# One core, two transformer layers: rotary keys transposed once, output weights packed, top-2 by ranks, last rows scaled by ScalarE

## The chip, the core and the metric

The kernel runs on one core of a Trainium2 chip. The metric is the device time of one execution in microseconds (us); less is better. PE is TensorE, ACT ScalarE, DVE VectorE, POOL GpSimd, and SP the engine that here only issues DMAs (SPq is its queue). Everything is float32 but for a few exact bf16 tables of the routing.

## The reference

640 token rows (128 context rows, then 512 latent rows) of 1024 columns pass two layers. What matters here, cut from the reference:

```python
def mix(qs, kvs, w_uk, w_uv, lam_p, diff_g, lam_init, w_out):
    k_nope = jnp.einsum('bkr,rhd->bkhd', ckv, w_uk)                    # 6 heads x 32
    k_a = jnp.concatenate([k_nope, jnp.broadcast_to(k_rope[:, :, None, :], ...)], axis=-1)  # + the same 32 for all heads
    ...                                                                # three kinds of attention
    return jnp.einsum('bse,ed->bsd', o, w_out)

def hier_moe(h, w_grp, b_grp, w_rtr, b_rtr, w_gate, w_up, w_down):
    g_top, g_idx = lax.top_k(jax.nn.softmax(t @ w_grp + b_grp), 1)     # one of 4 groups
    e_sel = ...                                                        # the 4 logits of that group
    e_top, e_idx = lax.top_k(jax.nn.softmax(e_sel), 2)                 # two of its 4 experts
    ...                                                                # 16 experts of 1024 -> 256 -> 1024
def block(...):
    mod = silu(cond) @ w_mod[i] + b_mod[i]                             # shift1, scale1, gate1, shift2, scale2, gate2
    h = rms_norm(x, norm1_g[i]) * (1 + scale1) + shift1
    x = x + gate1 * mix(...)
    h = rms_norm(x, norm2_g[i]) * (1 + scale2) + shift2
    x = x + gate2 * hier_moe(h, ...)
```

## The kernel before

Rows are worked on in NT = 5 tiles of 128. Each layer has five stages, written out by hand in program order for every engine, with semaphores between them.

1. **Projection** (`z_block`, `hT_round`, `keys1`, `keys2`). Per tile PE transposes the normalised rows (8 transposes, bank 7 of PSUM, L1799) and multiplies by `w_in` in four column blocks (L1907). Per unit of 128 keys (2 cached units and 5 of the tiles) `keys1` makes 4 transposes into bank 4, ACT copies them out (`key_copies_a`, L957 and L958), and `keys2` makes, for each of 3 head pairs, one product of `wuk` with the compressed keys (L1862) and one product of the raw key columns with the identity (L1863) that adds the rotary part in the same accumulation; ACT copies this out with one instruction of 128 partitions (L964).
2. **Attention**: scores, exponentials, transposes, values, by 10 map pairs per tile. Beside it PE makes the 8 later chunks of the modulation (`mod_chunk`, L1824) from 2 MB blocks of `w_mod`.
3. **Output projection** (`out_block`, L2098), in three column blocks of `w_out` per tile, with the residual add (`x_add`), the second norm (`mixer_in`) and the router logits. DVE's `mixer_in_last` makes the last tile's normalised rows (L1521), which POOL stores to `h_rows` in DRAM (L841).
4. **Routing**, on DVE: from the 20 logits per row the group, two experts, counts, ranks, slots (L1585 to L1680), with small products on PE in between. POOL then gathers the first 128 rows of `h_rows` (L893). In layer 0 PE also makes the four first modulation chunks of layer 1 and transposes their result (`mod_T`, L1840): chunks 0 and 1 ahead of the routing's counts, chunks 2 and 3 behind them, and then `mod_T`, ahead of the product that gives the slots (L2196).
5. **Experts**: steps of 128 gathered rows, 29 over both layers, of one expert or of two (gate and up L2248 to L2254, down L2289 to L2296). POOL adds each result to `x_rows` with a scatter that accumulates (L879), one at a time.

SBUF for weights is the `ring`, four slots of 2 MB, and the `arena`. SP issues all weight DMAs in one order (the list `USES`), each after a wait on what used the slot before (`slot_free`). Slot 3 also holds probabilities during attention. The three `w_out` blocks take slots 2, 0 and 1, one each; so chunk 0 of layer 1's modulation goes to slot 3 when attention is done, and chunks 1, 2 and 3 to slots 2, 0 and 1 as the last tile has used each `w_out` block. Experts 0 and 1 follow the chunks that they replace; experts 2 and 3 wait for the first gather besides. Softmax denominators of attention travel through DRAM (`fac_rows`) and come back, broadcast, into `q_tok[1]` or arena columns 4096 to 5120 (`factors_of`).

## Time and profile before

| what | value |
|---|---|
| time, median of 3 runs | 1405.07 us (1403.48 to 1409.73) |
| the profiled execution's own time | 1402.38 us |
| its span in the profile | 1400.6 us |
| mean granted clock of TensorE | 0.955 of full |
| PE busy | 1239.2 us, 88% of the span |
| DVE busy | 719.1 us, 51% |
| ACT busy | 412.7 us, 29% |
| POOL busy | 233.3 us, 17% |
| DMA | 250.48 MB, mean 179 GB/s |

The stages by the profile's clock: layer 0's projection runs from about 42 to 195 us, attention to 392, output projection to 473, routing to 506, experts to 717; layer 1's from 727 to 882, to 1076, to 1159, to 1185, and to the end. A busy share says how much an engine worked, not whether anyone waited for it. A busy engine in a stage of 99% is that stage's bound; in the routing all engines are mostly idle, and there the chain of waits tells what counts.

### The profile page before, as it was taken

What the parts mean: (1) busy time and instruction counts of PE and PEld (TensorE: products, weight loads), DVE (VectorE), ACT (ScalarE), POOL (GpSimd) and SP (SyncE); (2) the same over time, 40 slices, a digit from 0 to 9 for tenths busy, and PEclk for the clock granted to TensorE, in tenths of its full rate; (3) what the DMA queues carried; (4) which work ended last, traced back from release to release, by engine and by line L of the source; (5) the groups of instructions that cost most, each with busy time, mean ns of one, the idle gap of its engine ahead of it and who ended that gap; (6) DMA issues with size and microseconds to landing.
All of it is one profiled execution on the core that took longest, in us unless ns stands there. A gap on an engine that the chain in (4) does not pass through costs nothing.

```text
span 1400.6 us, 22064 instructions
## 1 busy us (share of the span) xinstructions
PE 1239.2 (88%) x7898; PEld 725.4 (52%) x7898; DVE 719.1 (51%) x1728; ACT 412.7 (29%) x931; POOL 233.3 (17%) x335
## 2 busy tenths in 40 slices
PE   4999999999989869988959999899998993999980
PEld 3455556767756534433435554676666662444330
DVE  0344436777834625553514453567786445455442
ACT  2111145766611201111111111567665110111101
POOL 1220021110121112211111001211111111111212
PEclk9899999999999979999969999999999996999995
DMA  9800188010052887999950005760113344899955
GB/s 346 303 15 1 62 302 240 17 47 17 16 177 80 318 358 262 351 375 358 312 174 14 1 1 180 271 153 16 48 31 97 130 153 167 325 372 367 336 179 181
DMA packets 75625, 250.48 MB, mean 179 GB/s; under 512 B 6551, under 2 KB 15392, under 8 KB 62896
## 3 DMA queue, kind: packets, MB, share of 16 engines
q1 hardware_dynamic: 56080, 183.26, 35.1%
q0 software_dynamic: 18976, 63.94, 15.9%
q8 instruction: 99, 1.62, 0.5%
q10 hardware_dynamic: 432, 1.36, 0.2%
q14 instruction: 38, 0.31, 0.1%
HBM read 219.12 MB, written 31.08 MB: 179 GB/s over the span
## 4 chain that ended last, share of the span: by engine, by line
PE 63%; DMA 20%; DVE 7%; issue 6%; DVEq 1%; ACT 1%; POOL 1%; SPq 0%; POOLq 0%; ACTq 0%
PE ps L1907 17%; DMA x_rows<-arena,idx 13%; PE ps L2098 10%; PE ps L1799 8%; PE ps L1981 8%; PE ps L2254 5%; PE ps L2034 5%; PE ps L1824 2%; PE ps L2296 2%; PE ps L2248 2%; DVE ring L1362 2%; DMA ring<-in_w_mod 2%; DMA ring<-in_w_in 1%; DMA x<-in_x_sample 1%; DMA hT_region<-h_rows,idx 1%
## 5 line engine op out<-in xcount | busy, mean ns | idle before, releaser
L1907 PE MATMUL ps<-ring,hT_region 128*128 128x512 f32 (+1 forms) x640 | 270.3, 578 | 3.4 <-ACT hT_region L990 3.4
L1907 PEld LDWEIGHTS ps<-ring,hT_region 128*128 128x128 f32 x640 | 120.9, 192 | 134.4 <-issue 133.9
L1362 DVE TENSOR_SCALAR_CACHE_REDUCE ring<-ps 128x768 f32<-128x768 f32 (+1 forms) x168 | 132.7, 820 | 95.5 <-PE ps L1981 77.6
L1044 ACT ACTIVATE ring<-ring,negm 128x768 f32<-128x768 f32 (+1 forms) x168 | 137.6, 820 | 26.8 <-DVE ring L1362 26.8
L2098 PE MATMUL ps<-ring,hT_region 128*128 128x384 f32 (+1 forms) x480 | 143.5, 454 | 0.0
L2254 PE MATMUL ps<-ring,hT_region 128*128 x272 | 127.2, 623 | 10.3 <-SPq L600 4.3
L1981 PE MATMUL ps<-arena,qT 64*128 64x384 f32 (+1 forms) x640 | 124.8, 507 | 8.5 <-DVE ring L1362 4.1
L2098 PEld LDWEIGHTS ps<-ring,hT_region 128*128 128x128 f32 x480 | 89.2, 190 | 42.9 <-issue 1.5
L2034 PE MATMUL ps<-work,arena 128*64 128x128 f32 x1600 | 105.0, 278 | 5.6 <-ACT work L1060 4.3
L1060 ACT ACTIVATE work<-ps 128x512 f32<-128x512 f32 x128 | 75.8, 592 | 89.1 <-PE ps L1799 89.1
L2034 PEld LDWEIGHTS ps<-work,arena 128*64 128x64 f32 x1600 | 85.9, 136 | 24.6 <-issue 14.3
L2248 PE MATMUL ps<-ring,hT_region 128*64 x192 | 88.2, 614 | 9.8 <-SPq L600 9.8
L879 POOL DMA_INDIRECT x_rows<-arena,idx x29 | 47.9, 1652 | 293.9 <-DVE arena L1771 205.1
L2254 PEld LDWEIGHTS ps<-ring,hT_region 128*128 128x128 f32 x272 | 53.4, 199 | 80.6 <-issue 80.6
L1149 ACT ACTIVATE work<-ps 128x256 f32<-128x256 f32 x29 | 11.2, 384 | 281.8 <-PE ps L2254 158.9
L1758 DVE COPY work<-ps 128x256 f32<-128x256 f32 x29 | 12.3, 424 | 158.9 <-PE ps L1799 158.9
L2249 PE MATMUL ps<-ring,hT_region 128*64 128x512 f32 x192 | 88.3, 614 | 0.0
L1799 PE MATMUL ps<-ident,ring 128*128 128x128 f32 x600 | 81.9, 278 | 0.3
L1799 PEld LDWEIGHTS ps<-ident,ring 128*128 128x128 f32 x600 | 65.2, 140 | 28.0 <-issue 25.1
L1981 PEld LDWEIGHTS ps<-arena,qT 64*128 64x128 f32 (+1 forms) x640 | 56.1, 185 | 41.7 <-issue 15.0
L1237 DVE TENSOR_TENSOR work<-ps,rope 128x256 f32<-128x256 f32 (+2 forms) x40 | 14.0, 350 | 114.4 <-PE ps L1907 113.5
L1824 PE MATMUL ps<-ring,silu_c 128*2 128x128 f32 x1536 | 51.0, 290 | 19.9 <-DMA ring<-in_w_mod 19.2
(305 smaller groups left out, 1724.3 us busy)
## 6 DMA issues: line engine op xcount, KB each, us to landing
ring<-in_w_mod SPq DMA_DIRECT2D x24, 2048.0 KB, 10.5
ring<-in_moe_w_gate SPq DMA_DIRECT2D x32, 1024.0 KB, 11.6
ring<-in_moe_w_up SPq DMA_DIRECT2D x32, 1024.0 KB, 15.2
arena<-in_moe_w_down SPq DMA_DIRECT2D x32, 1024.0 KB, 14.3
ring<-in_w_in SPq DMA_DIRECT2D x6, 2048.0 KB, 20.2
arena<-mod_rows POOLq DMA_DIRECT2D x12, 512.0 KB, 5.7
arena<-fac_rows POOLq DMA_DIRECT2D x20, 256.0 KB, 4.4
x_rows<-x POOLq DMA_DIRECT2D x10, 512.0 KB, 3.1
```

The lines of the kernel that those rows point to most:

```text
L1044: act.activation(v, v, ACT.Exp, bias=negm[:, 2 * (k % 3) + m:2 * (k % 3) + m + 1], scale=-1.0, accum_out=sums[:, c:c + 1]).then_inc(exp_do ...
L1060: act.activation(to[:, 512 * b:512 * (b + 1)], ps[:, 4 + b, :], ACT.Copy).then_inc(pt_evac[b], 1)
L1362: ts(o_, i_, -pair_of(p)[4], None, ALU.mult, ALU.min, accum_out=col).then_inc(m_ready, 1)
L1799: return pe.transpose(out, in_, ident[:])
L1824: last = mm(ps[32 * h:32 * h + 2, mod_bank(j), mod_cols(j)], silu_v[:, :, c], w[:, c, 128 * h:128 * (h + 1)], start=(c == 0), stop=(c == K ...
L1907: last = mm(ps[:, b, 0:n], hT[:, c, t * P:(t + 1) * P], w[:, c, :], start=(c == 0), stop=(c == KC - 1))
L1981: last = mm(ps[:, 2 * m + c, 0:384], q[r:r + n, :], kT[r:r + n, plane, 384 * c:384 * (c + 1)], start=True, stop=True)
L2034: last = mm(ps[64 * m:64 * (m + 1), 7, (u % 4) * P:(u % 4 + 1) * P], V[:, s_, vc:vc + 64], w[:, 768 * m + c * P:768 * m + (c + 1) * P], st ...
L2098: last = mm(ps[:, n % 4, 0:w_], oT[:, c, t * P:(t + 1) * P], w[:, c, :], start=(c == 0), stop=(c == KC - 1))
L2248: mm(g[0:HALF], h[:, c, 0:HALF], wa[:, c, :], start=(c == 0), stop=(c == KC - 1))
L2249: last = mm(g[HALF:P], h[:, c, HALF:P], wb[:, c, :], start=(c == 0), stop=(c == KC - 1))
L2254: last = mm(g, h[:, c, :], wa[:, c, :], start=(c == 0), stop=(c == KC - 1))
```

## The change

- **Rotary transposes joined.** `keys1` makes a fifth transpose, of the raw key columns with the rotary part, into bank 7; `key_copies_a` writes it to all three head pairs with two ACT copies of 32 partitions (rows 32 and 96), and a new semaphore `kr_evac` guards bank 7 ahead of `hT_round`. The three identity products of `keys2` are gone. `key_copies_b` copies the product's rows 0 and 64, 32 partitions each, where it was one copy.
- **Output weights packed.** The three `w_out` blocks lie one behind the other in slots 0 and 1. Slot 2 is free once attention's chunks are done, slot 3 with attention's end. `LATE`, the order in which experts take slots, is now 2, 3, 0, 1. Layer 1's chunks 0 to 3 lie in slots 2 and 3 and in two places of the arena (`mod_home`) that held keys, values and queries. Factors come back to the last 1024 columns of the weights for the keys (`factors_of`), and small tiles of the router move to make room.
- **Loads.** `first_experts` replaces the list's order: gate and up of expert 2 after the next-to-last block of the output projection; experts 0 and 1 after chunks 0 and 1 (in layer 1: expert 0's gate and up before attention ends, the rest of 0 and 1 at its end); expert 2's down and all of 3 after the first gather, as before.
- **Top-2 by ranks.** Each set of 4 logits is compared with itself, all pairs at once (25 sets x 16 = 400 elements), against a table `above` made once, and the sum gives each logit's place. The gate weights are computed behind the expert table and no longer ahead of it. A running sum (one `tensor_tensor_scan`) replaces product and reduction over 16 x 16.
- **Last rows.** `mixer_in_last` is gone. POOL writes the shift row (`b2b`) to the last tile of `h_rows` early; ACT scales the last rows; POOL adds them to that tile in DRAM with an accumulating DMA, ahead of the last `x_store`.

The diff, cut:

```diff
+        uses += [("out", l, b, b) for b in range(len(WO_COLS))]
+            uses += [("mod", l + 1, j, (2, 3, 1, 0)[j]) for j in range(MOD_FIRST)]
...
+        def wo_block(b):
+            return ring[:, WO_AT[b]:WO_AT[b] + KC * (WO_COLS[b][1] - WO_COLS[b][0])].rearrange("p (c n) -> p c n", c=KC)
+        def mod_home(l, j):
+            if l >= 1 and j in (2, 3):
+                return arena[:, DN0 + 4096 * (3 - j):DN0 + 4096 * (4 - j)]
+            return slot[USES[USE_AT["mod", l, j]][3]]
...
+                elif kind == "mod" and l >= 1:
+                    if i == 0:
+                        sp.wait_ge(mod_done, l * N_MOD - 2)
+                    else:
+                        sp.wait_ge(pv_done, l * NUT)
...
 for t in range(NT):
+                    if t == 1:
+                        pool.wait_ge(s_bcast, (l + 1) * 32)
+                        dma(h_rows[NT * P:(NT + 1) * P, :], b2b[:, 1, :]).then_inc(s_hout, 16)
...
+                pool.wait_ge(h2_ready, l * NT + NT)
+                dma(h_rows[NT * P:(NT + 1) * P, :], h2, accum_op=ALU.add).then_inc(s_hout, 16)
                 x_store(NT - 1)
-                h2_store(NT - 1)
                 pool.wait_ge(idx_ready, l + 1)
-                pool.wait_ge(s_hout, l * 80 + 80)
+                pool.wait_ge(s_hout, l * 96 + 96)
...
 def key_copies_a(l, u):
+                for r in (32, 96):
+                    last = act.activation(kT[r:r + 32, 0:3, KCOL[u]:KCOL[u] + P],
+                                          ps[r:r + 32, 7, 0:P].unsqueeze(1).to_broadcast([32, 3, P]), ACT.Copy)
+                last.then_inc(kr_evac, 1)
 def key_copies_b(l, u):
-                act.activation(kT[:, 0:3, KCOL[u]:KCOL[u] + P],
-                               ps[:, 5, 0:384].rearrange("p (j n) -> p j n", j=3), ACT.Copy)
+                for r in (0, 64):
+                    act.activation(kT[r:r + 32, 0:3, KCOL[u]:KCOL[u] + P],
+                                   ps[r:r + 32, 5, 0:384].rearrange("p (j n) -> p j n", j=3), ACT.Copy)
...
+                act.wait_ge(lg_ready, l * NT + NT)
+                act.wait_ge(s_hout, l * 96 + 16 * NT)
+                act.activation(h2, last_scaled, ACT.Copy, scale=rs2[:, NT - 1:NT]).then_inc(h2_ready, 1)
                 act.wait_ge(r_sub, 2 * l + 1)
                 act.activation(r_gex, r_gs, ACT.Exp).then_inc(r_exp, 1)
-                act.wait_ge(r_sub, 2 * l + 2)
-                act.activation(r_ex2, r_d, ACT.Exp).then_inc(r_exp, 1)
                 if l + 1 < DEPTH:
                     for j in range(MOD_FIRST):
                         mod_copy(l + 1, j)
+                act.wait_ge(r_sub, 2 * l + 2)
+                act.activation(r_ex2, r_d, ACT.Exp).then_inc(r_exp, 1)
...
+                tt(beats, four.unsqueeze(2).to_broadcast([P, blocks_, 4, 4]),
+                   four.unsqueeze(3).to_broadcast([P, blocks_, 4, 4]), ALU.subtract)
+                tt(beats, beats, above[:]..., ALU.is_ge)
+                red(v3(r_place, 4), beats, AX.X, ALU.add)
+                ts(r_first, r_place, 0.0, None, ALU.is_equal)
+                ts(r_second, r_place, 1.0, None, ALU.is_equal)
...
+                dve.tensor_tensor_scan(r_incl, ones[:, 0:NE], r_nt, 0.0, ALU.mult, ALU.add)
...
 def keys1(l, u):
+                pe.wait_ge(kr_evac, l * NU + u)
+                if u == 0 and l >= 1:
+                    pe.wait_ge(a1_ready, l + 1)
+                tr(ps[:, 7, 0:P], kt[:, 128:256])
 def keys2(l, u):
                 for j in range(3):
-                    mm(ps[:, 5, j * P:(j + 1) * P], wuk[:, j * P:(j + 1) * P], ckvT[:], start=True, stop=False)
-                    mm(ps[:, 5, j * P:(j + 1) * P], kt[:, 128:256], ident[:], start=False, stop=True)
+                    mm(ps[:, 5, j * P:(j + 1) * P], wuk[:, j * P:(j + 1) * P], ckvT[:], start=True, stop=True)
 def hT_round(t, r):
+                    if r == 0:
+                        pe.wait_ge(kr_evac, l * NU + (t + 1 if t or l else 2))
```

How the order moves. First PE in the projection of layer 0, over one key unit: `keys1` (four L1799 on `pack`, between two blocks), then `keys2`. Before:

```order
L1799 MATMUL ps<-ident,pack 128x128 x4
L1907 MATMUL ps<-ring,hT_region 128x416 x8
L1799 MATMUL ps<-ident,work 128x128 x4
L1907 MATMUL ps<-ring,hT_region 128x512 x8
L1862 MATMUL ps<-ckvT,pack 128x128
L1863 MATMUL ps<-ident,pack 128x128
L1862 MATMUL ps<-ckvT,pack 128x128
L1863 MATMUL ps<-ident,pack 128x128
L1862 MATMUL ps<-ckvT,pack 128x128
L1863 MATMUL ps<-ident,pack 128x128
L1864 MATMUL ps<-pack,ckvT 128x384
```

And after the change, the same stretch (L1838 is the transpose, L1949 the block, L1903 and L1904 are `keys2`):

```order
L1838 MATMUL ps<-ident,pack 128x128 x5
L1949 MATMUL ps<-ring,hT_region 128x416 x8
L1838 MATMUL ps<-ident,work 128x128 x4
L1949 MATMUL ps<-ring,hT_region 128x512 x8
L1903 MATMUL ps<-ckvT,pack 128x128 x3
L1904 MATMUL ps<-pack,ckvT 128x384
```

Of each unit three of the seven products of `keys2` are gone, and `keys1` has five transposes where it had four. Second, SP's queue in layer 0 from `w_out` to the experts, with its waits. Before:

```order
L657 DMA ring<-in_w_out 128x2x256
L603 DMA ring<-in_w_mod 128x8x512 [waits pv_done,z_done]
L603 DMA ring<-in_w_mod 128x8x512 [waits wo_done] x3
L575 DMA ring<-in_moe_w_gate 128x2048 [waits mod_done]
L575 DMA ring<-in_moe_w_up 128x2048
L579 DMA arena<-in_moe_w_down 128x2048 [waits pv_done]
L575 DMA ring<-in_moe_w_gate 128x2048 [waits mod_done]
L575 DMA ring<-in_moe_w_up 128x2048
L579 DMA arena<-in_moe_w_down 128x2048
L575 DMA ring<-in_moe_w_gate 128x2048 [waits experts_ready,wgu_landed0,wd_landed0,wgu_landed1,wd_landed1,mod_done,s_hg0_0]
L575 DMA ring<-in_moe_w_up 128x2048
L579 DMA arena<-in_moe_w_down 128x2048
```

After the change:

```order
L617 DMA ring<-in_w_mod 128x8x512 [waits w_landed2,mod_done]
L617 DMA ring<-in_w_mod 128x8x512 [waits pv_done]
L617 DMA arena<-in_w_mod 128x8x512 [waits w_landed1,pv_done]
L617 DMA arena<-in_w_mod 128x8x512 [waits w_landed0,pv_done]
L589 DMA ring<-in_moe_w_gate 128x2048 [waits wo_done]
L589 DMA ring<-in_moe_w_up 128x2048
L589 DMA ring<-in_moe_w_gate 128x2048 [waits mod_done]
L589 DMA ring<-in_moe_w_up 128x2048
L589 DMA ring<-in_moe_w_gate 128x2048 [waits mod_done]
L589 DMA ring<-in_moe_w_up 128x2048
L593 DMA arena<-in_moe_w_down 128x2048 [waits mod_done]
L593 DMA arena<-in_moe_w_down 128x2048
```

The loads of chunks 1 to 3 no longer wait for the output projection (`wo_done`), expert 2's gate and up stand ahead of expert 0's, and the two downs behind both. Third, DVE in the routing of layer 0, from the last step of the selection to the counts. Before:

```order
L1604 TENSOR_TENSOR arena<-arena 128x5x4x4 x2
L1607 TENSOR_TENSOR arena<-arena 128x80
L1609 TENSOR_TENSOR arena<-lane 128x256
L1521 SCALAR_TENSOR_TENSOR work<-arena,small 128x1024
L1614 TENSOR_SCALAR arena<-ps 128x16
L1616 TENSOR_SCALAR arena<-arena 128x16
L1619 TENSOR_TENSOR arena<-arena 128x256
L1621 TENSOR_SCALAR arena<-arena 128x8
L1622 TENSOR_SCALAR arena<-arena 128x8
L1624 TENSOR_REDUCE arena<-arena 128x16
L1626 CAST arena<-arena 128x8
```

After the change, the whole selection from its first instruction (L1627) to the running sum (L1653) that stands for L1619 and L1624:

```order
L1627 TENSOR_TENSOR arena<-work 128x400
L1630 TENSOR_TENSOR arena<-arena,above 128x400
L1633 TENSOR_REDUCE arena<-arena 128x100
L1635 TENSOR_SCALAR arena<-arena 128x100
L1636 TENSOR_SCALAR arena<-arena 128x100
L1640 TENSOR_TENSOR arena<-arena 128x5x4x4 x2
L1643 TENSOR_TENSOR arena<-arena 128x80
L1645 TENSOR_REDUCE arena<-work 128x5
L1647 TENSOR_TENSOR arena<-work,arena 128x20
L1649 TENSOR_SCALAR arena<-ps 128x16
L1651 TENSOR_SCALAR arena<-arena 128x16
L1653 SCALAR_TENSOR_TENSOR arena<-ones,arena 128x16
```

The 1024-column instruction L1521 is gone from this queue. Ahead of the mask's sum (L1607 before, L1643 now) the selection has seven instructions, three of which read 400 elements; before it had 22, of 5 to 80 elements.

## Rows read from the trace of the kernel before

**Rows 1.** The chain that ended last: shares of the span by engine.

```profile
PE 63%; DMA 20%; DVE 7%; issue 6%; DVEq 1%; ACT 1%; POOL 1%; SPq 0%; POOLq 0%; ACTq 0%
```

**Rows 2.** Windows: from:to, length, busy per engine (count), PE clock, DMA share, GB/s.

```profile
60.00:195.00 135.00, 133.47 (x468) 68.35 (x470) 64.44 (x215) 19.66 (x56) 19.02 (x26) 1.00 0.18 62
398.00:473.00 75.00, 74.04 (x352) 50.46 (x352) 33.33 (x55) 9.40 (x20) 13.13 (x26) 1.00 0.38 133
483.00:493.00 10.00, 6.04 (x96) 4.63 (x90) 6.08 (x29) 2.16 (x8) 0.15 (x1) 0.81 1.02 423
...
600.00:700.00 100.00, 87.30 (x333) 35.94 (x330) 47.69 (x69) 13.53 (x20) 16.47 (x13) 0.97 0.98 349
...
1168.00:1177.00 9.00, 0.78 (x15) 0.46 (x11) 7.86 (x35) 0.00 (x0) 0.53 (x1) 0.50 0.16 61
```

**Rows 3.** Timeline (start us, length us, engine, line), PE, `keys2` of one unit.

```profile
179.84 0.38 PE L1862 MATMUL ps<-ckvT,pack 128*128 128x128 f32 x2
...
180.06 0.39 PE L1863 MATMUL ps<-ident,pack 128*128 128x128 f32 x2
```

**Rows 4.** Timeline, PE: twelve transposes of attention in one row.

```profile
374.87 1.53 PE L1799 MATMUL ps<-ident,ring 128*128 128x128 f32 x12
```

**Rows 5.** Timeline, PE and ACT, projection of layer 0: `keys1` to `hT_round`.

```profile
78.47 0.60 PE L1799 MATMUL ps<-ident,pack 128*128 128x128 f32 x4
...
79.28 0.48 ACT L958 ACTIVATE arena<-ps 128x384 f32<-128x384 f32 x1
...
79.66 1.06 ACT L950 ACTIVATE work<-x 128x1024 f32<-128x1024 f32 x1
...
84.50 0.60 PE L1799 MATMUL ps<-ident,work 128*128 128x128 f32 x4
```

**Rows 6.** Timeline, DVE, the routing of layer 1.

```profile
1161.35 0.24 DVE L1539 SCALAR_TENSOR_TENSOR work<-ps,small,pack 128x20 f32<-128x20 f32 x1 [0.98 <-POOL small L722]
...
1167.08 0.24 DVE L1607 TENSOR_TENSOR arena<-arena 128x80 bf16<-128x80 f32 x1
...
1168.78 0.17 DVE L1614 TENSOR_SCALAR arena<-ps 128x16 f32<-128x16 f32 x1
...
1169.27 0.43 DVE L1619 TENSOR_TENSOR arena<-arena 128x256 f32<-128x256 f32 x1
...
1170.41 0.17 DVE L1626 CAST arena<-arena 128x8 int32<-128x8 f32 x1
...
1176.86 0.18 DVE L1680 SCALAR_TENSOR_TENSOR idx<-arena,w_slot 128x18 int32<-128x18 f32 x1
```

**Rows 7.** Chain (start us, length us, what), the first gather of layer 1.

```profile
1177.32 4.36 DMA hT_region<-h_rows,idx
```

**Rows 8.** Line 879, scatters that add: issue to landing.

```profile
DMA to landing us min/median/max: 6.0/10.8/12.1
```

**Rows 9.** Line 841, plain stores of rows: issue to landing.

```profile
DMA to landing us min/median/max: 2.9/2.9/8.6
```

**Rows 10.** Timeline, SP queue, layer 0: chunks 1 to 3, then expert 0.

```profile
460.41 11.49 SPq L603 DMA_DIRECT2D ring<-in_w_mod  x3
475.85 0.35 SPq L575 DMA_DIRECT2D ring<-in_moe_w_gate  x1
```

**Rows 11.** Chain, the routing of layer 0, to the first expert step.

```profile
485.70 3.51 PE ps L1824 x64
...
490.40 1.05 PE ps L1840 x8
...
493.80 8.63 DMA hT_region<-h_rows,idx
...
506.58 3.54 PE ps L2254 x4
```

**Rows 12.** Timeline, DVE and PE, routing of layer 0: last logits, then chunk 2.

```profile
474.56 0.24 DVE L1539 SCALAR_TENSOR_TENSOR work<-ps,small,pack 128x20 f32<-128x20 f32 x1 [0.98 <-POOL small L722]
...
481.19 1.93 PE L1824 MATMUL ps<-ring,silu_c 128*2 128x128 f32 x64
```

More of the change, by code:

```diff
@@ L85 @@
 WO_COLS = [(0, 384), (384, 768), (768, 1024)]
+WO_AT = [KC * c0 for c0, _ in WO_COLS]
 RING = 4
@@ L154 @@
 USE_AT = {u[:3]: g for g, u in enumerate(USES)}
-SLOT_AT = {u[:3]: u[3] for u in USES}
-USE_BEFORE = [max((h for h in range(g) if USES[h][3] == u[3]), default=None) for g, u in enumerate(USES)]
 USE_CUM = [16 * sum({"moe": 0, "out": 4}.get(v[0], 1) for v in USES[:g + 1] if v[3] == u[3])
@@ L1464, in _ @@
                     if t == NT - 1:
+                        if p == 0 and l == 0:
+                            rank_table()
                         if p == 1:
@@ new lines, in _ @@
+                four = logits.rearrange("p t n -> p (t n)").rearrange("p (b n) -> p b n", n=4)
+                beats = r_big[:, 0:blocks_ * 16].rearrange("p (b i j) -> p b i j", i=4, j=4)
+                tt(beats, four.unsqueeze(2).to_broadcast([P, blocks_, 4, 4]),
+                   four.unsqueeze(3).to_broadcast([P, blocks_, 4, 4]), ALU.subtract)
+                dve.drain()
+                tt(beats, beats, above[:].rearrange("p (i j) -> p i j", i=4).unsqueeze(1).to_broadcast([P, blocks_, 4, 4]),
+                   ALU.is_ge)
@@ new lines, in _ @@
+                dve.drain()
+                red(v3(r_place, 4), beats, AX.X, ALU.add)
+                dve.drain()
+                ts(r_first, r_place, 0.0, None, ALU.is_equal)
+                ts(r_second, r_place, 1.0, None, ALU.is_equal)
+                dve.drain()
+                first, second = (v.rearrange("p (t b n) -> p t b n", t=NT, n=4) for v in (r_first, r_second))
+                for o_, O_ in ((first, r_O1), (second, r_O2)):
+                    tt(O_.rearrange("p (t e g) -> p t g e", t=NT, e=EPG), o_[:, :, 1:, :],
+                       first[:, :, 0, :].unsqueeze(3).to_broadcast([P, NT, NGRP, EPG]), ALU.mult)
@@ L1606, in _ @@
-                dve.drain()
-                tt(r_Mb, r_O1, r_O2, ALU.add).then_inc(r_mask, 1)
-                tt(r_le.rearrange("p (e s) -> p e s", e=NE), lane[:, 0:NE].unsqueeze(2).to_broadcast([P, NE, NE]),
-                   lane[:, 0:NE].unsqueeze(1).to_broadcast([P, NE, NE]), ALU.is_ge)
-                mixer_in_last()
+                tt(v3(r_gs, 4), G, r_gm.unsqueeze(2).to_broadcast([P, NT, 4]), ALU.subtract).then_inc(r_sub, 1)
                 dve.wait_ge(r_count, l + 1)
@@ L1703, in _ @@
                    ).then_inc(experts_ready, 1)
+                for k, O_ in enumerate((r_O1, r_O2)):
+                    tt(r_sel[:, 80 * k:80 * (k + 1)].rearrange("p (t e g) -> p t g e", t=NT, e=EPG),
+                       E.rearrange("p t (g e) -> p t g e", g=NGRP),
+                       O_.rearrange("p (t e g) -> p t g e", t=NT, e=EPG), ALU.mult)
+                dve.drain()
+                red(r_m, v3(r_sel, NE), AX.X, ALU.add)
+                dve.drain()
+                tt(r_d, r_m[:, NT:2 * NT], r_m[:, 0:NT], ALU.subtract).then_inc(r_sub, 1)
+                dve.wait_ge(r_exp, 2 * l + 1)
+                red(r_gtop, v3(r_gex, 4), AX.X, ALU.add)
+                dve.wait_ge(r_exp, 2 * l + 2)
+                ts(r_den, r_ex2, 1.0, None, ALU.add)
                 dve.drain()
```

205 lines of the change are left out of this document (95 added, 110 removed).

## The prediction

> **What bounds the kernel now.** I read the chain that ended last first: PE holds 63% of it and DMAs 20% [rows 1]. Then the windows, stage by stage [rows 2]. In layer 0's projection PE is busy 133.47 of 135 us, in the output projection 74.04 of 75: there every product that goes is time that goes. In the output projection the DMA engines are at 0.38, so loads fit in. The routing is the opposite: in 9 us of layer 1's routing PE works 0.78 us and DVE 7.86, at a granted clock of 0.50, the lower of the two levels (1.2 GHz), after PE had gone idle. There the length of DVE's chain is the time. In layer 0's routing the DMA engines are full too (1.02, 423 GB/s), with PE busy 6.04 of 10 us at 0.81. In the experts stage PE is busy 87.30 of 100 us and the DMA engines 0.98: both are near their limit.
>
> **Rotary transposes.** In `keys2` a pair of records starts every 0.22 us [rows 3]; three identity products are 0.66 us a unit. What comes is one transpose: twelve take 1.53 us with a tail of about 0.28, so (1.53 - 0.28) / 11 = 0.11 us each [rows 4]. Net 0.55 us a unit. Units 0 and 1 of layer 0 lie ahead of the first block, which waits for weights, and unit 0 of layer 1 under the load of x; that leaves 5 + 6 = 11 units in a PE-bound stretch: -6.1 us. The new copies are ACT's, which is busy 19.66 of 135 us [rows 2]. A copy of as many columns (384) takes 0.48 us [rows 5]; I take 32 partitions for no cheaper than 128. After `key_copies_a` two more end at about 79.76 + 2 x 0.48 = 80.7 us, and the next user of bank 7, `hT_round`, starts at 84.50 [rows 5]: 3.8 us of cover, which a block of `w_in` gives. Behind them on ACT the square sum (79.66, 1.06 us) starts 0.9 us later; it is for the tile after next. If ACT were late, PE would stand at every unit.
>
> The Trainium skill (TensorE: Matmul & The Clock Gate, Part 4: PE-mode transpose) gives about 275 ns for a transpose in one kernel's context. This trace has records of that length but starts them every 0.11 us [rows 4]; by the page's figure the net would be 0.39 us a unit and the sum 1.8 us smaller.
>
> **Routing, layer 1.** From the start of the last logits instruction to the end of the mask's sum (L1607) are 1167.32 - 1161.35 = 5.97 us [rows 6], of which 0.33 is the first instruction. The new selection: a 256-element instruction takes 0.43 us, and a small one 0.17 [rows 6], so 400 elements are about 0.43 + 144 x 1.1 ns = 0.58. Three of these, each with 0.07 for the drain, 1.95; two of 100 elements 0.36; two of 80 0.47; the sum 0.24: 3.0 us against 5.64, so -2.6. Then L1609 and L1521 stood ahead of the counts, which begin 1168.78 - 1167.32 = 1.46 us behind the mask [rows 6]; now two small ones stand there and PE's five small products, about 0.5: -1.0. From the counts to the cast 1170.41 - 1168.78 = 1.63 us go to product, reduction and four small ones [rows 6]. The trace has no running sum; bounds are a small instruction (0.17) and a 256-element one (0.43). I take 0.2, since it has 16 elements: 0.94 in all, -0.7, ends -0.7 and -0.4. Joining two products and two reductions gives -0.1. Together **-4.4 us**. Behind the expert table DVE has about 1.6 us more for the weights; the gather's 4.36 us [rows 7] and PE's transposes cover it, with some 0.7 us to spare.
>
> The last rows now go ACT, POOL, DMA. ACT can start at 1161.6, takes about 1.06 (1024 columns, [rows 5]), and POOL issues near 1163.0. No row shows a plain add into DRAM. Nearest are the scatters that add: 6.0 us at the least, 12.1 at the most [rows 8]; a plain store needs 2.9, and 8.6 under load [rows 9]. The DMA engines are nearly idle here, so I take 6.0: landed at 1169, ahead of the gather's new issue at 1177.3 - 4.4 = 1172.9. With 12.1 it would cost 2.2 us. It can't gain.
>
> **Routing, layer 0.** SP issued chunks 1 to 3 from 460.41 to 471.90 [rows 10], 6.3 MB, and experts 0 and 1, 6.3 MB, from 475.85. Chunk 3's products could therefore start only at 485.70, `mod_T` at 490.40, and the gather was issued at 493.80 [rows 11]. Now the chunks are loaded as attention ends, some 60 us early, while PE has the output projection. Next in line: the mask at 474.56 + 0.33 + 3.0 = 477.9 [rows 12], `r_gs` and its exponential 0.6, the copy of chunk 0 (about 1.1), chunk 2 (1.93, [rows 12]), chunk 3, its copy: `mod_T` starts near 484.9, -5.5 us, and still ends behind DVE's tables (-4.4). So the gather is issued near 488.3. It took 8.63 us here against 4.36 in layer 1 [rows 7, 11]. From 475.85 on there are 6.3 MB of experts 0 and 1 and four row tiles of 0.5 MB, 8.4 MB, at 420 GB/s [rows 2] 20 us: about 495.9. Between 492.7 (4.36) and 496.9 (8.63) I take 495.9, near the loaded row. Before, it had landed at 502.43: **-6.5 us**, ends -5.5 and -9.8. The adding DMA is issued near 476.2; with 12.1 us it lands at 488.3, just in time.
>
> The Trainium skill (DMA: Bandwidth & Descriptors, Queues, rings and completion order) says that an engine takes turns between queues packet by packet. By that what counts is whether the weights' queue has work, not how much: the gather would keep its 8.63 us, and the sum be 1.0 us smaller.
>
> **The rest.** Expert 2's gate and up are loaded before the routing, but PE reached step 2 without waiting, so I cost this at nothing; steps follow at PE's pace. The packed `w_out` does not change a product. The table of ranks is two small instructions in late attention, with what DVE delays there +0.3 us. More bytes early in the output projection (6.3 MB in layer 0, 4.2 in layer 1, 10 to 15 us) lie beside the factors' return; cover is PE's 74 us.
>
> Sum: -6.1 - 4.4 - 6.5 + 0.3 = **-16.7 us**. The profiled execution's own time of 1402.4 gives 1385.7; it is 2.7 us under the median of 1405.07, so for the median I say **1388.4 us**.
>
> **Rivals.**
> 1. *Bytes bind the experts.* For it: DMA share 0.98 at 349 GB/s [rows 2]. Then layer 0 gains the 6.3 MB that leave the crowded time, 18 us, and layer 1 another 2.1 MB, 6 us, in place of 6.5 and 4.4: 1388.4 - 13.1 = 1375. Against it: PE is busy 87.30 of the same 100 us.
> 2. *Routing half won.* The adding DMA needs 12 us in layer 1 and more in layer 0, where stores triple under load [rows 9], and the gather waits for it: 2.2 and about 4 us lost, 1394.6.
> 3. *The joined transposes don't shorten the projection*, since PE waits for ACT at bank 7. The 3.8 us of cover speak against it. Without the 6.1 us: 1394.5.
> 4. *Slower: the adding DMA is late in both layers.* With a landing L after issues at 476.2 and 1163.0, the gathers move by 2L - (493.8 - 476.2) - (1177.3 - 1163.0) = 2L - 31.9 us. With the other terms (-5.8) it is slower from L = 18.9; L = 24 gives +10.3, 1415. For it: a read, an add and a write of DRAM, beside full engines in one layer. Against it: 12.1 is the longest of 29 [rows 8].
>
> **How the numbers follow.** Forecast 0.70, rival 1 0.08, rival 2 0.13, rival 3 0.05, rival 4 0.04. A measurement tells 0.5%, 7 us, from no change. The forecast's own ends: routing of layer 0 -9.8 gives 1385, the transposes' page figure, 12.1 in layer 1 and the running sum's 0.3 and 1.0 for layer 0's gather give 1393.7. Rivals 2 and 3 reach from 1394 to 1397 with part of each other, rival 1 halfway 1380; the range is 1380 to 1397. Over 7 us faster: forecast, rival 1 and most of 2 and 3, 0.88. Within: 0.08, the rest of them. Slower: 0.04.
>
> **What would show it.** Right: projection stages each about 3 us shorter with PE still at 99%; no DMA wait ahead of chunk 3; counts about 3.6 us sooner behind the last logits; the gather in layer 1 issued 4.4 us sooner; experts stages as long as before. Wrong: PE waiting on ACT ahead of `hT_round`; POOL's gather released by the adding DMA rather than by DVE; an experts stage that changes its length by several us.

## The result and the profile after

The changed kernel took **1390.37 us** (median of 4 runs, 1387.05 to 1392.83), the kernel before beside it 1404.28 us. The ratio is 0.9893, 95% interval 0.9868 to 0.9917: 13.9 us faster, by more than the 0.5% that a measurement can tell. The prediction was 1388.4 us, 1380 to 1397.

The profiled execution took 1392.47 us, of which the span is 1390.7. I cut the span at the first product of each stage, and at the end of the last tile's last output block. "Again" is the same changed kernel, profiled a second time (e9_again below). All numbers are durations in us between two such starts in the timeline:

| stretch | before | after | again |
|---|---|---|---|
| start to first `w_in` block | 42.62 | 43.04 | 42.94 |
| layer 0: projection, to the first wide scores | 171.99 | 172.74 | 168.80 |
| rest of attention | 177.83 | 179.58 | 178.19 |
| output projection, to the end of its last block | 78.90 | 78.58 | 78.68 |
| routing, to the first expert product | 35.24 | 29.72 | 30.03 |
| experts | 220.94 | 219.60 | 222.26 |
| layer 1: projection and attention | 352.80 | 349.04 | 349.14 |
| output projection | 77.81 | 77.66 | 77.64 |
| routing | 27.21 | 22.80 | 22.72 |
| experts and end | 215.26 | 217.94 | 218.10 |

Read it downwards: both routings became shorter, and so did the projections, but for layer 0's in the first execution; layer 1's experts became longer in both executions. In layer 0's projection and attention the two executions of one and the same kernel differ by 5.3 us.

The chain of waits of the changed kernel, its share by engine; it answers to [rows 1]:

```profile
PE 71%; DMA 13%; DVE 6%; issue 5%; ACT 1%; DVEq 1%; POOL 1%; SPq 1%; POOLq 0%; ACTq 0%
```

A key unit in the projection, timeline (start us, duration, engine, line, operation, tiles):

```profile
79.54 0.71 PE L1838 MATMUL ps<-ident,pack 128*128 128x128 f32 x5
...
80.46 0.48 ACT L997 ACTIVATE arena<-ps 128x384 f32<-128x384 f32 x1
...
80.97 0.98 ACT L1001 ACTIVATE arena<-ps 32x384 f32<-32x384 f32 x2
...
81.97 1.06 ACT L989 ACTIVATE work<-x 128x1024 f32<-128x1024 f32 x1
...
85.68 0.60 PE L1838 MATMUL ps<-ident,work 128*128 128x128 f32 x4
```

`keys1` has five transposes. The two new ACT copies (L1001) end at 81.95, `hT_round` starts at 85.68 right behind the block before it, with no wait: 3.7 us of cover, as [rows 5] had let expect. A copy of 32 partitions takes 0.49 us, no less than one of 128. Block starts in layer 1's projection gain 0.57 us per unit.

DVE in layer 1's routing (answers to [rows 6]):

```profile
1153.19 0.24 DVE L1592 SCALAR_TENSOR_TENSOR work<-ps,small,pack 128x20 f32<-128x20 f32 x1 [0.98 <-POOL small L757]
...
1156.39 0.24 DVE L1643 TENSOR_TENSOR arena<-arena 128x80 bf16<-128x80 f32 x1
...
1157.06 0.17 DVE L1649 TENSOR_SCALAR arena<-ps 128x16 f32<-128x16 f32 x1
...
1157.56 0.19 DVE L1653 TENSOR_TENSOR_SCAN arena<-ones,arena 128x16 f32<-128x16 f32 x1
...
1157.96 0.17 DVE L1657 CAST arena<-arena 128x8 int32<-128x8 f32 x1
...
1164.27 0.18 DVE L1710 SCALAR_TENSOR_TENSOR idx<-arena,w_slot 128x18 int32<-128x18 f32 x1
```

From last logits to the end of the mask are 3.44 us (5.97 before); the counts begin 0.43 us behind it (1.46); the running sum takes 0.19 us and counts to cast 0.90 (1.63).

Layer 0's routing, POOL and PE in the timeline, then the pieces of the chain of waits, and last how long the adding DMA took to land (layer 1, mean, layer 0):

```profile
478.89 0.97 POOL L899 DMA_DIRECT2D h_rows<-work  x1 [1.83 <-ACT work L1172]
...
482.35 3.68 PE L1863 MATMUL ps<-arena,silu_c 128*2 128x128 f32 x128 [1.02 <-ACT modrow L976]
...
487.26 2.13 PE L1879 MATMUL ps<-ident,modrow 2*128 2x2 f32 x16 [1.23 <-ACT modrow L976]
...
490.71 1.09 POOL L932 DMA_INDIRECT hT_region<-h_rows,idx  x1 [10.28 <-DVE idx L1710]
...
499.62 1.97 PE L1838 MATMUL ps<-ident,hT_region 128*128 128x128 f32 x8 [8.04 <-DMA hT_region<-h_rows,idx]
```

```profile
490.71 8.86 DMA hT_region<-h_rows,idx
503.66 9.70 PE ps L2296 x16
```

```profile
1164.73 4.37 DMA hT_region<-h_rows,idx
```

```profile
DMA to landing us min/median/max: 5.4/8.1/10.9
```

PE goes from the counts into chunks 2 and 3 without a DMA wait, `mod_T` starts at 487.26, and the gather is issued at 490.71. It takes 8.86 us here and 4.37 in layer 1, as before ([rows 7, 11]). The adding DMA landed 10.9 us after its issue at 478.89, at 489.79, which is 0.92 us ahead of the gather. That is no slack of 0.9 us: where the gather waited for the last rows (e2, e6, e10, e11 and e12 below), POOL issued it 0.83 to 0.84 us after they had landed. So here the transfer would have allowed the gather at 490.63, 0.08 us before DVE's index did; in the second execution it is 0.24 us. In layer 1 the adding DMA took 5.4 us and was far from the path.

### The profile page after: what moved, and what is told of

Same layout as the page of the kernel before. It is cut to its first block, busy times and chain, and to the rows that moved or that the text cites. A ratio compares the mean times of both kernels' runs of the same rounds, so it can differ in the third digit from the quotient of the medians.

```text
span 1390.7 us, 21925 instructions
## 1 busy us (share of the span) xinstructions
PE 1236.9 (89%) x7828; PEld 720.1 (52%) x7828; DVE 714.1 (51%) x1702; ACT 437.3 (31%) x975; POOL 234.9 (17%) x337
## 4 chain that ended last, share of the span: by engine, by line
PE 71%; DMA 13%; DVE 6%; issue 5%; ACT 1%; DVEq 1%; POOL 1%; SPq 1%; POOLq 0%; ACTq 0%
PE ps L1949 19%; PE ps L2140 10%; PE ps L1838 9%; DMA x_rows<-arena,idx 8%; PE ps L2023 8%; PE ps L2296 6%; PE ps L2076 5%; PE ps L2290 4%; PE ps L2338 3%; PE ps L1863 3%; DVE ring L1409 2%; DMA ring<-in_w_mod 2%; PE ps L2331 1%; DMA arena<-in_moe_w_down 1%; DMA hT_region<-h_rows,idx 1%
## 5 line engine op out<-in xcount | busy, mean ns | idle before, releaser
L1949 PE MATMUL ps<-ring,hT_region 128*128 128x512 f32 (+1 forms) x640 | 271.3, 580 | 3.4 <-ACT hT_region L1034 3.4
L1949 PEld LDWEIGHTS ps<-ring,hT_region 128*128 128x128 f32 x640 | 121.2, 193 | 135.1 <-issue 134.6
L2296 PE MATMUL ps<-ring,hT_region 128*128 x272 | 128.9, 629 | 10.3 <-SPq L614 4.5
L1838 PE MATMUL ps<-ident,ring 128*128 128x128 f32 x600 | 82.3, 279 | 0.3 <-ACT work L1100 0.2
L1838 PEld LDWEIGHTS ps<-ident,ring 128*128 128x128 f32 x600 | 65.4, 141 | 28.0 <-issue 25.1
L2338 PE MATMUL ps<-arena,work 128*128 x136 | 67.2, 640 | 1.7 <-DVE work L1797 1.7
```

Source lines behind the costliest of these rows:

```text
L1838: return pe.transpose(out, in_, ident[:])
L1949: last = mm(ps[:, b, 0:n], hT[:, c, t * P:(t + 1) * P], w[:, c, :], start=(c == 0), stop=(c == KC - 1))
L2296: last = mm(g, h[:, c, :], wa[:, c, :], start=(c == 0), stop=(c == KC - 1))
L2338: last = mm(ps[:, 5 + k, :], h[:, c, :], wa[:, c, k * 512:(k + 1) * 512], start=(c == 0), stop=(c == 1))
```

## The experiments

Unless said otherwise each is the changed kernel with one edit; the diffs are cut. The kernel before was measured beside e1 to e4, beside e5 to e8 and beside e9 to e12, and took 1404.03, 1402.70 and 1404.12 us, so ratios to it compare better than medians. The bracket behind a ratio is its 95% interval.

**e1: rotary part undone.**

```diff
-                tr(ps[:, 7, 0:P], kt[:, 128:256])
...
+                    mm(ps[:, 5, j * P:(j + 1) * P], kt[:, 128:256], ident[:], start=False, stop=True)
```

> The changed kernel with its rotary part undone: three identity products per unit in `keys2`, no fifth transpose, no `kr_evac`, one copy of 128 partitions. My theory: each of 11 units in a PE-bound stretch gets 0.55 us back, so +6.1 us on the changed kernel's 1390.4: 1396.5 us, and the granted clock at the start of layer 0's attention falls here as well, or in neither, since it isn't tied to the transposes. Rival A: the fall of the granted clock at 201 to 221 us (about 3.8 us in the profiled execution) comes with the joined transposes; then undoing them costs only 6.1 - 3.8, about 1392.7 us, and the windows from 201 to 221 us show a clock of 1.0. Rival B: PE waited for the new copies all the same; then nothing is lost, 1390.4.

1396.69 us, ratio 0.9928 (0.9908 to 0.9949): +6.3 on the changed kernel's median, 4.9 by the ratios, whose intervals overlap by 0.0009. The trace decides: in layer 1 the starts of the tiles' blocks are 29.49 us apart, as in the kernel before, where the changed kernel has 28.93: 0.56 us per unit. Rival B falls. The granted clock fell to 0.50 at 213 to 217 us here too, so that fall doesn't hang on the joined transposes: rival A falls.

**e2: last rows undone.**

```diff
-                act.activation(h2, last_scaled, ACT.Copy, scale=rs2[:, NT - 1:NT]).then_inc(h2_ready, 1)
...
-                dma(h_rows[NT * P:(NT + 1) * P, :], h2, accum_op=ALU.add).then_inc(s_hout, 16)
...
+                mixer_in_last()
                 dve.wait_ge(r_count, l + 1)
```

> The changed kernel with the last rows as before: DVE scales and shifts them (`mixer_in_last`, behind the mask and ahead of the counts), POOL stores them plainly behind the last `x_store`, no early store of the shift row. My theory: DVE's instruction delays the counts by 1.0 us; in layer 1 that is 1.0 us on the path, in layer 0 DVE's tables end 1.8 us ahead of `mod_T`'s end, so nothing: 1391.4 us, +1.0. Rival: the adding DMA and the extra store of 512 KB per layer slow the first gather by a microsecond or more; then this kernel is faster than the changed one, by 1 us or more, and its gathers in the trace take less than 8.86 and 4.37 us.

1391.54 us, 0.9898 (0.9877 to 0.9918). Not told apart from the changed kernel; the rival expected it faster, for which there is no sign in the time. The rival's other sign did come in layer 0, where the gather took 7.60 us; but it was issued 2.1 us later, counted from the end of the last output block, and landed 0.8 us later than in the changed kernel. The trace says where the part works. Layer 1's routing is 23.84 us, +1.04 as expected. Layer 0's is 30.58, +0.9, where I expected nothing:

```profile
482.30 0.53 POOL L876 DMA_DIRECT2D h_rows<-work  x1 [4.80 <-DVE work L1567]
...
490.09 0.18 DVE L1708 SCALAR_TENSOR_TENSOR idx<-arena,w_slot 128x18 int32<-128x18 f32 x1
...
492.62 1.09 POOL L928 DMA_INDIRECT hT_region<-h_rows,idx  x1 [9.79 <-DMA h_rows<-work]
```

and from the chain of waits of the same profile:

```profile
482.30 9.49 DMA h_rows<-work
...
492.62 7.60 DMA hT_region<-h_rows,idx
```

DVE's index is ready at 490.27, but POOL issues the gather at 492.62, 0.83 us after the plain store has landed, which took 9.49 us. So ACT's scaling is worth something in layer 0 because it starts the transfer 3.4 us sooner.

**e3: chunks loaded late.**

```diff
-                        sp.wait_ge(pv_done, l * NUT)
+                        sp.wait_ge(wo_done, (l - 1) * 15 + 3 * (NT - 1) + i)
...
-                    gate_up_of(l, 2)
...
+                    gate_up_of(l, 2)
```

> The changed kernel with the loads of layer 1's chunks 0 to 3 issued as late as before (chunk 0 at the end of attention, chunks 1 to 3 as the last tile has used one `w_out` block each), and expert 2's gate and up behind the first gather again in layer 0. Places stay. My theory: chunk 3 is late again, `mod_T` and the gather in layer 0 move back by 5.5 us, and the gather keeps its 8.6 to 8.9 us: +5.5, 1396 us. Rival (bytes): less is in flight when the gather runs, or more, and the gather's length changes by 1 us or more; +4.5 or +6.5. Rival (nothing): layer 0's path goes over DVE's chain, which is as short as in layer 1, and the loads were not what bound; +0, 1390.

1397.87 us, 0.9946 (0.9925 to 0.9967): +7.5, by the ratios 7.4. PE in layer 0:

```profile
489.20 3.59 PE L1862 MATMUL ps<-arena,silu_c 128*2 128x128 f32 x64 [5.87 <-DMA arena<-in_w_mod]
494.02 2.13 PE L1878 MATMUL ps<-ident,modrow 2*128 2x2 f32 x16 [1.23 <-ACT modrow L975]
```

Chunk 3 waits 5.87 us for its weights and runs at half clock after that wait. The stretch from the end of the last output block to the first expert product is 36.29 us, +6.6, and longer than the 35.24 of the kernel before. The gather took 7.78. Without the early loads nothing of the gain in layer 0's routing is left; the loads are worth more there than my 5.5.

**e4: old selection.**

```diff
-                tt(beats, beats, above[:]..., ALU.is_ge)
-                red(v3(r_place, 4), beats, AX.X, ALU.add)
...
+                first_of(G, r_gm, r_og)
...
+                first_of(v3(r_es, 4), r_m1, r_o1)
...
+                first_of(v3(r_es2, 4), r_m2, r_o2)
```

> The changed kernel with the old selection (`first_of` three times: group, first and second expert) in place of the places by comparison; the gate weights stay behind the expert table, the scan and the rest stay. My theory: last logits to mask grow by 2.5 us; in layer 1 all of it is on the path; in layer 0 the counts' products stand on PE ahead of chunks 2 and 3, so `mod_T` moves by about 1.3 us, and DVE's tables (1.8 us of room) by 2.5: +1.3. Sum +3.8, 1394.2 us. Rival: layer 0 hides it all, +2.5, 1392.9.

1396.10 us, 0.9938 (0.9918 to 0.9958): +5.7. Layer 1's routing is 25.20 us, +2.4 as expected. Layer 0's is 32.35, +2.6 and not +1.3:

```profile
476.69 0.28 PE L2235 MATMUL ps<-arena,ones_b 128*128 128x16 bf16 x5 [3.24 <-DVE arena L1659]
...
478.12 5.27 PE L1877 MATMUL ps<-arena,silu_c 128*2 128x128 f32 x128 [0.77 <-ACT modrow L977]
```

PE waits 3.24 us for the mask (0.53 in the changed kernel), and chunks 2 and 3 take 5.27 us in place of 3.68, at a mean granted clock of 0.69. Both my cases lacked that. It is not shown that the longer wait is the cause. In the kernel before PE waited as long for its mask, and chunk 2 right behind it took 1.93 us [rows 12], its length at full clock:

```profile
480.60 0.28 PE L2179 MATMUL ps<-arena,ones_b 128*128 128x16 bf16 x5 [3.07 <-DVE arena L1607]
```

And in e5 and e8 below the two chunks took 5.32 and 5.30 us after waits no longer than the changed kernel's.

**e5: weights held back in layer 0.**

```diff
-                    for e in range(2):
-                        sp.wait_ge(mod_done, at + e + 1)
-                        gate_up_of(l, e)
...
+                    sp.wait_ge(mod_done, at + 1)
+                    gate_up_of(l, 0)
...
                 sp.wait_ge(s_hg[l][0], 16)
+                    down_of(l, 0)
+                    gate_up_of(l, 1)
+                    down_of(l, 1)
```

> The changed kernel, but in layer 0 SP issues expert 1's gate and up and the downs of experts 0 and 1 only when the first gather has landed; layer 1 as it is. Turn-taking theory (the gather took 8.86 us with weights in flight and 4.37 without, whatever the number of bytes): the gather takes 4.4 to 5 us, the first step starts 4 us sooner, 1386.4 us, if what is loaded later isn't missed. Rival (the path only moves): the first two steps then wait for 3 to 4 MB of weights, some 8 to 10 us at 420 GB/s, and give back what the gather gains, or more: 1390 to 1395 us, with DMA waits ahead of the first steps' downs or of the second step. Rival (bytes, other traffic): the gather keeps 7 us or more although no weights are in flight.

**1382.86 us, 0.9854 (0.9832 to 0.9876)**, 7.5 us under the changed kernel by the medians, 5.5 by the ratios, and the fastest of all. Its interval lies below that of the changed kernel's second measurement (e9) and overlaps with the first one's by 0.0008.

```profile
481.25 5.32 PE L1868 MATMUL ps<-arena,silu_c 128*2 128x128 f32 x128 [1.02 <-ACT modrow L981]
...
491.20 1.09 POOL L937 DMA_INDIRECT hT_region<-h_rows,idx  x1 [11.86 <-DVE idx L1715]
...
495.61 1.97 PE L1843 MATMUL ps<-ident,hT_region 128*128 128x128 f32 x8 [3.54 <-DMA hT_region<-h_rows,idx]
```

With no weights in flight the gather takes 4.4 us. The routing is 26.80 us though the clock had fallen and chunks 2 and 3 took 5.32 us. Experts of layer 0 take 219.86 us (219.60): nothing is given back. Both rivals fall, and the turn-taking theory's 4.4 us is what came; that the number of bytes doesn't matter is more than this run tests. The trace accounts for 2.9 us in the routing. Where the rest of the 5.5 to 7.5 us comes from isn't located, and e11, which holds back the same weights, is only 2 to 4 us under the changed kernel.

**e6: `mod_T` behind the slots' product.**

```diff
-                    mod_T(l + 1)
...
                 for k in range(2 * NT):
...
                 last.then_inc(r_rows, 1)
+                if l + 1 < DEPTH:
+                    mod_T(l + 1)
```

> The changed kernel, but PE makes `mod_T` of layer 1 behind the products that give slots and expert table, not ahead of them. My theory: in layer 0 the slots' product starts when DVE's tables are ready (487.6 us in the changed kernel's trace, against 489.3), so the gather is issued 1.7 us sooner: 1388.7 us, -1.7. Rival: what bounds the gather's end is not its issue (the rows of weights in flight end at the same time), or `mod_T` between table and gather delays something else: 0. Both expect no move in layer 1.

1389.93 us, 0.9902 (0.9868 to 0.9935): no difference.

```profile
478.19 0.98 POOL L899 DMA_DIRECT2D h_rows<-work  x1 [1.83 <-ACT work L1172]
...
487.65 0.18 DVE L1710 SCALAR_TENSOR_TENSOR idx<-arena,w_slot 128x18 int32<-128x18 f32 x1
...
490.30 1.09 POOL L932 DMA_INDIRECT hT_region<-h_rows,idx  x1 [10.56 <-issue]
```

The index is ready at 487.83, the gather goes out at 490.30. The profile names no releaser; the adding DMA, issued at 478.19, landed after 11.3 us, 0.84 us ahead of the gather, and in e11 below it is named. Neither expectation had it: the gather's next limit is that transfer.

**e10: e6 and e2 together.**

> Both single edits at once: `mod_T` behind the slots' product, and the last rows scaled by DVE and stored plainly. Alone the first moved DVE's index 2.6 us forward in layer 0, but POOL issued the gather 2.47 us behind it, when the adding DMA had landed (about 12 us after its issue). Theory (the adding DMA is what the gather waited for there): POOL now issues the gather within 0.5 us of the index; layer 0 is 0.7 to 1 us faster than the changed kernel, layer 1 1.0 us slower, sum about 0. Rival (under these loads a plain store lands no sooner: 8.6 us from about 481.7 us is 490.3): the gather still waits 1 us or more behind the index, and layer 0 gains nothing.

1390.43 us, 0.9894 (0.9869 to 0.9919). In the trace the index is ready at 486.15 and the gather is issued at 489.05, released by the plain store. The rival is right: under these loads a plain store lands in 9.45 us, an adding DMA in 10.5 to 11.5 (the profiles of the other kernels), and what the store gains in length it loses by its later start.

**e11: e5, e6, and the last `x_store` behind the first gather.**

> Held weights as in e5_hold (layer 0), `mod_T` behind the slots' product, and the last `x_store` behind the first gather. In e5_hold the gather was issued 18.4 us behind the start of the last output block's product; DVE's index would now be ready 14.6 us behind it, and the adding DMA, with 0.5 MB less beside it, lands between 15.5 and 17. Theory: 1.4 to 2.8 us faster than e5_hold, about 1381 us. Rival (the adding DMA alone sets its 11 us, whatever runs beside it): 1 us or less, 1382 us.

1388.13 us, 0.9872 (0.9849 to 0.9896).

```profile
477.02 0.97 POOL L904 DMA_DIRECT2D h_rows<-work  x1 [1.83 <-ACT work L1178]
...
486.48 0.18 DVE L1716 SCALAR_TENSOR_TENSOR idx<-arena,w_slot 128x18 int32<-128x18 f32 x1
...
488.89 1.12 POOL L936 DMA_INDIRECT hT_region<-h_rows,idx  x1 [10.90 <-DMA h_rows<-work]
```

The adding DMA took 11.0 us without the store beside it, and the gather waited for it again: the rival has the mechanism right. The routing is 25.93 us, 0.9 less than in e5, but the time isn't better than e5's, and both numbers missed; the intervals overlap.

**e7: PE kept busy at the start.**

```diff
                 mod_chunk(0, j)
+                if j < MOD_FIRST - 1:
+                    for _ in range(6 if j == 1 else 24):
+                        tr(ps[:, 0, 0:P], ident[:])
```

> The changed kernel with unused transposes of the identity on PE at the start: 6 between chunks 1 and 2 and 24 (2.6 us at 0.11 us each) between chunks 2 and 3, where PE waits 4.03 us for weights; results go to a bank that nobody reads. Theory (the joined transposes leave PE idle for longer ahead of chunk 3, the granted clock falls there to half, and chunk 3 takes 3.60 us, not 1.93): with the filler chunk 3 takes 1.93 us and the first block starts 1.7 to 2.5 us sooner: 1388.4 us. Rival (the clock is at half there from other causes; in the kernel before it was, too, with 2.25 us of idle time): chunk 3 stays at 3.4 to 3.6 us and the filler gains nothing or costs up to 1 us. Whether the granted clock still falls at 200 to 220 us is looked at as well; if that fall hangs on when the stages start, it can go or stay.

1395.05 us, 0.9936 (0.9913 to 0.9959): slower than the changed kernel by the medians, though the intervals overlap with those of both its measurements (by 0.0004 and 0.0014), and not faster. Chunk 3 in the changed kernel, then e7:

```profile
32.49 3.60 PE L1863 MATMUL ps<-ring,silu_c 128*2 128x128 f32 x64 [4.03 <-DMA ring<-in_w_mod]
```

```profile
28.68 2.84 PE L1838 MATMUL ps<-ident 128*128 128x128 f32 x24
32.28 1.93 PE L1863 MATMUL ps<-ring,silu_c 128*2 128x128 f32 x64 [0.76 <-DMA ring<-in_w_mod]
...
41.16 15.61 PE L1952 MATMUL ps<-ring,hT_region 128*128 128x512 f32 x32 [1.69 <-ACT hT_region L1034]
```

Chunk 3 takes 1.93 us and the first block starts 1.9 us sooner, as the theory had it; the clock stayed at 1.00 from 201 to 221 us as well. One profile can't price the filler, though: e1 and e4, without it, had chunk 3 at 1.93 us and the first block at 40.9 and 41.1 us too, where the wait for weights happened to be 2.56 and 1.25 us. And in layer 1 the clock fell (0.83 in the ten us from 880), and projection and attention there took 352.1 us in place of 349.0. That is 3 us; where the rest of the loss comes from stays open.

**e8: PE kept busy in the routing.**

```diff
+                for _ in range(48 if l == 0 else 24):
+                    tr(ps[:, 4, 0:P], ident[:])
                 def slot_weights():
```

> The changed kernel with unused transposes of the identity on PE behind the expert table, where it waits for the first gather: 48 in layer 0, 24 in layer 1, 0.11 us each at the full clock, 0.22 at half. Theory (the first step's transposes and products run at half clock only because PE was idle before, and this time is on the path): the step's first 16 products take 7.0 us, not 9.7, and the transposes 1.0, not 2.0: 3.6 us a layer, 1383.2 us. Rival (PE's idle time ends too late for it, or the step's weights bind it): the clock is still 0.5 when the step starts, +0 to -2 us. Rival (the filler runs past the gather's landing): up to 2 us longer a layer.

1389.57 us, 0.9909 (0.9888 to 0.9930): no difference. Layer 1:

```profile
1166.34 5.38 PE L1838 MATMUL ps<-ident 128*128 128x128 f32 x24
1171.51 1.16 PE L1838 MATMUL ps<-ident,hT_region 128*128 128x128 f32 x8
1173.72 7.13 PE L2299 MATMUL ps<-ring,hT_region 128*128 x16 [1.06 <-DVE hT_region L1774]
```

There the theory holds in the trace: transposes 1.16 us (1.97), first 16 products 7.13 (9.65), although PE starts about 1.6 us behind the gather's landing; from the expert table's product to the end of the step's gate and up it is 2.4 us less. In layer 0 chunks 2 and 3 took 5.30 us, the gather 10.3 us, PE was idle for 2.7 us again, and the routing was 32.76 us, 3.0 longer than in the changed kernel. Both rivals had a part of it.

**e12: e11 with 18 transposes per layer.**

> The kernel of e11_hold_modT with 18 unused transposes on PE between the expert table and the first gather's rows in both layers (24 in layer 1 overshot the landing by about 1.5 us in e8_fill_routing and yet shortened the stretch up to the first step's end by 2.4 us). Theory: the granted clock rises before or in the first step in both layers; 2 to 3 us each, about 1376 us. Rival (18 are too few: the clock rises as late as without them): no more than 1 us of gain, 1380 us.

1385.95 us, 0.9874 (0.9838 to 0.9910). The runs spread over 14 us.

```profile
1164.91 1.16 PE L1844 MATMUL ps<-ident,hT_region 128*128 128x128 f32 x8 [0.23 <-DMA hT_region<-h_rows,idx]
1168.67 10.01 PE L2306 MATMUL ps<-ring,hT_region 128*128 x16 [2.60 <-issue]
```

In layer 1 the transposes ran at full clock, but then PE stood for 2.60 us (1.63 in the changed kernel), the last 1.53 of it behind DVE's copy and for nothing that the profile shows, and the products took 10.01 us. The theory's 1376 us fails; no gain over e11 that is clear of the noise is seen.

**e9: the changed kernel again.**

> The changed kernel itself once more, to know its spread beside the other kernels of this call: 1390.4 us, between 1387 and 1393 as in its first four runs. Theory (the granted clock falls to half at a place in attention in some executions and not in others): the runs again lie in two groups some 4 to 5 us apart, the slower with the lower mean clock. Rival: one group only.

1391.69 us, 0.9903 (0.9879 to 0.9927), runs from 1387.58 to 1395.49 with no gap between them: one group, the theory of two falls. But the ten runs of this kernel sort by their mean clock: 0.953 to 0.956 below 1391.1, 0.948 to 0.953 above. The profiles show one place of it, by 4 us (columns: stretch, its length, busy us and instructions of PE, PEld, DVE, ACT, POOL, granted clock, DMA share, GB/s). First execution:

```profile
201.00:205.00 4.00, 3.79 (x54) 2.38 (x58) 0.67 (x6) 2.30 (x10) 0.43 (x1) 0.58 1.05 391
...
213.00:217.00 4.00, 3.83 (x16) 2.55 (x16) 2.01 (x9) 1.81 (x7) 0.00 (x0) 0.50 0.30 113
```

Again:

```profile
201.00:205.00 4.00, 3.86 (x83) 2.82 (x82) 0.84 (x9) 2.83 (x13) 0.38 (x1) 1.00 1.04 373
...
213.00:217.00 4.00, 4.00 (x82) 2.53 (x84) 3.40 (x11) 1.95 (x4) 0.30 (x1) 1.00 0.13 28
```

Same program, same stretch: 0.50 against 1.00. Of the 13 profiles of the changed kernel and its versions, ten have a clock under 0.9 in 200 to 210 or 210 to 220 us, three (e4, e7, e9) in neither, and the kernel before has none there. What decides it stays open.

## Why the prediction was right, and where not

- **Rotary transposes, -6.1.** Right. 0.57 us per unit; the projections' stretches in the second execution are 3.2 and 3.7 us shorter, e1 costs 6.3 by the medians and 4.9 by the ratios. The cover of 3.7 us held (rival 3 falls). The first execution hides it in layer 0 behind the clock's fall. The Trainium skill (TensorE: Matmul & The Clock Gate, Part 4: PE-mode transpose) would have given an estimate of 0.39 us a unit by its 275 ns; the trace doesn't agree with that for this stretch, and the measured spacing decides.
- **Routing of layer 1, -4.4.** Right to the tenth: -4.4 and -4.5. Selection -2.5 (forecast -2.6; e4 gives 2.4), `mixer_in_last` -1.0 (e2), counts to cast -0.73 (-0.7), the scan 0.19 us (0.2). The adding DMA took 5.4 us (6.0 were taken).
- **Routing of layer 0, -6.5.** Too large: -5.5 and -5.2. The issue moved by 5.7 us as forecast 5.5. The term that was mis-sized is "About 495.9", the gather's length worked out from bytes: it took 8.86 and 9.18 us, not 7.6. My own lower end came nearer: the weights' queue had work until after the gather had landed, and e5 shows the other side, 4.4 us without weights in flight. By the rule of the Trainium skill (DMA: Bandwidth & Descriptors, Queues, rings and completion order) whether that queue has work is what counts, and the traces agree so far. They don't agree that the length then stays the same: it was 10.3 us in e8, and in e2, e3, e4 and e10, where the gather was issued 2 to 8 us later, 7.3 to 7.8 us, with experts 0 and 1 still landing until 0.3 to 0.5 us before it. A gather that starts later ends with the bytes, as I had worked it out; this one didn't.
- **The adding DMA, "with 12.1 us it lands at 488.3, just in time".** Just in time it was, with 10.9 us, but closer than that reads: the sum had no term for the 0.84 us from landing to the gather's issue. Rival 2 missed by 0.08 us in one execution and 0.24 in the other, so that it lost there is partly luck. What I hadn't seen is that a plain store, which here starts some 3.5 us later, would be no better (9.5 us).
- **The rest, +0.3.** Wrong by some 2.5 us. Layer 1's experts and end are 2.7 and 2.8 us longer. The stall of the next section is about 1.1 us of it; 1.6 and 1.8 us arise before it, 0.7 and 0.8 of them in the first step, and their cause stays open. Over all the profiles this stage took 213.5 to 219.7 us, so a part may be chance. Layer 0's experts stage moved by -1.3 and +1.3 us; rival 1 wanted a gain of 18 us in layer 0 and falls.
- **The sum.** -16.7 was forecast for the profiled execution, -9.9 and -12.1 came; median against median it is -13.9. Terms on the path were right within 1.3 us; layer 1's experts cost 2.7, and two executions of the changed kernel differ by up to 5.3 us in one stretch. That the time came within 2.0 us of 1388.4 is partly luck: the gain by the medians was 2.8 us smaller than forecast, and the kernel before came out at 1404.28 us beside it, 0.8 lower than the 1405.07 that I started from.
- **The parts.** Undone one at a time they cost 6.3, 1.2, 7.5 and 5.7 us (e1 to e4), 20.7 together, against 13.9 for the whole. In layer 0's routing e2, e3 and e4 cost 0.9, 6.6 and 2.6 us where the whole gained 5.5: the parts lie on one path there, and each is worth more once the others are in place.

## What the runs showed that I had not expected

**A stall that goes with the length of PE's program.** In the last expert step PE waits before two small transposes although DVE's input is long there. The changed kernel, then e8:

```profile
1351.90 0.67 PE L1838 MATMUL ps<-ident,work 128*128 128x128 f32 x2 [2.42 <-issue]
1353.36 6.37 PE L2338 MATMUL ps<-arena,work 128*128 x8 [0.79 <-DVE work L1797]
```

```profile
1347.78 0.48 PE L1838 MATMUL ps<-ident,work 128*128 128x128 f32 x2 [0.40 <-DVE work L1790]
1349.59 3.69 PE L2341 MATMUL ps<-arena,work 128*128 x8 [1.33 <-DVE work L1797]
```

In the first, PE stood 2.42 us for nothing that the profile shows, and the products behind it took 6.37 us, against 3.69 in e8 and 5.39 in the kernel before, which has no such wait. All the profiles of programs with 7828 PE products (the changed kernel, twice, and e2, e3, e4, e5, e6, e10, e11) have this wait, of 2.4 to 3.0 us; those with 7858 (e7), 7864 (e12), 7898 (before, e1) and 7900 (e8) have 0.39 to 0.49, for DVE or just behind it. Adding 30, 36 or 72 useless transposes elsewhere takes it away. It costs less than it lasts: from its start to the end of the span are 41.2 us in the changed kernel, 40.2 in the kernel before and 39.9 in e8. The steps that aren't used are jumped over just there, and the Trainium skill (Runtime: NRT & Kernel Launch, Instruction fetch mechanics) says that a taken branch to a page of code that isn't loaded makes the engine wait for it. The pattern agrees, but no run shows the fetch as the cause: the trace has the transfers of instructions as queues of their own, and between 1348 and 1352 us it shows no transfer at all.

**A wait can cost more than its length.** Behind waits of 3 to 6 us (e3, e4, chunk 3 at the start) PE ran at or near half clock for a while, and a chunk or a pair of chunks took 1.6 to 1.7 us more. But the length of the wait alone doesn't settle it: 3.07 us in the kernel before left chunk 2 at full clock, and in e5 and e8 the clock fell behind waits of 0.5 and 1.0 us. These runs don't show which waits are paid twice.
